# A four-layer FP32 model on one core: VectorE in place of GpSimd makes the low part of each FFN step's product

## The reference

```python
def conv_ffn(h, w_in, conv_w, conv_b, w_out):
    z = causal_dwconv(h @ w_in, conv_w, conv_b)
    u, g = jnp.split(z, 2, axis=-1)
    return (jax.nn.gelu(g) * u) @ w_out
```

```python
    h = rms_norm_2(x, g_ffn)
    a = depthwise_conv(h @ w_ffn_gate, conv_w, conv_b)
    x = x + (jax.nn.gelu(a) * (h @ w_ffn_up)) @ w_ffn_down
```

## Time and profile before

| what | value |
|---|---|
| median of 3 runs | 1607.45 us (1607.23 to 1610.52) |
| the profiled execution, its own time | 1609.04 us |
| its span, first to last instruction | 1607.2 us |
| TensorE matmuls, busy | 1558.6 us, 97% |
| VectorE, busy | 1139.6 us, 71% |
| ScalarE, busy | 908.7 us, 57% |
| GpSimd, busy | 163.4 us, 10%, of which y_lo<-qk 112.5 us in 53 instructions (44 of them in the FFNs) |
| granted clock of TensorE, mean | 0.990 |

### The profile page before, as it was taken

How to read it: one execution, slowest core, us unless ns; L and a number is a source line. 1 busy time by engine, 2 the same in 40 slices (tenths; PEclk the granted TensorE clock), 3 DMA queues, 4 the chain that set the end, 5 groups by cost and what they waited for, 6 DMA issues and landing times.

```text
span 1607.2 us, 30225 instructions
## 1 busy us (share of the span) xinstructions
PE 1558.6 (97%) x12828; PEld 1507.2 (94%) x12828; DVE 1139.6 (71%) x1366; ACT 908.7 (57%) x1207; POOL 163.4 (10%) x94
## 2 busy tenths in 40 slices
PE   7889999998899999999999999998999999999998
PEld 7879999998899999899899999998989989999998
DVE  6638876877888777768647876668677647777566
ACT  6436645677757656646554744456645645645444
POOL 0130112101012110000012010010000012010010
PEclk9989999999999999999999999999999999999999
DMA  9325555444455545432335455544533234565552
GB/s 319 114 83 186 197 188 176 165 142 141 146 183 185 205 164 187 155 131 103 111 124 182 147 205 183 195 172 153 188 133 106 106 106 141 181 210 183 183 186 76
DMA packets 38268, 258.73 MB, mean 161 GB/s; under 512 B 4752, under 2 KB 5392, under 8 KB 7568
## 3 DMA queue, kind: packets, MB, share of 16 engines
q1 hardware_dynamic: 37728, 255.33, 45.8%
q10 hardware_dynamic: 432, 1.84, 0.3%
HBM read 256.10 MB, written 1.05 MB: 160 GB/s over the span
## 4 chain that ended last, share of the span: by engine, by line
PE 77%; issue 10%; DVE 6%; ACT 5%; POOL 1%; DMA 1%; SPq 0%; POOLq 0%; ACTq 0%; DVEq 0%
PE bank L1610 23%; PE bank L1612 22%; PE bank L1611 22%; PE bank L1887 3%; PE bank L1846 3%; DVE w_lo L948 2%; ACT w_hi L474 2%; PE bank L1865 2%; PE bank L1792 1%; DVE qk L1339 1%; PE bank L1819 1%; PE bank L1989 1%; DMA raw<-W 1%; POOL y_lo L1534 1%; DVE h_lo L963 1%
## 5 line engine op out<-in xcount | busy, mean ns | idle before, releaser
L1610 PE MATMUL bank<-h_hi,w_hi 128*128 128x256 f32 x2640 | 751.8, 285 | 19.2 <-DVE h_lo L963 14.7
L1612 PE MATMUL bank<-h_hi,w_lo 128*128 128x256 f32 x2640 | 741.9, 281 | 0.0
L1611 PE MATMUL bank<-h_lo,w_hi 128*128 128x256 f32 x2640 | 741.9, 281 | 0.0
L948 DVE TENSOR_TENSOR w_lo<-raw,w_hi 128x2048 fp32r<-128x2048 f32 x238 | 553.9, 2329 | 199.2 <-ACT w_hi L474 198.3
L474 ACT ACTIVATE w_hi<-raw 128x2048 fp32r<-128x2048 f32 x238 | 455.0, 1912 | 251.8 <-PE bank L1612 250.1
L1610 PEld LDWEIGHTS bank<-h_hi,w_hi 128*128 128x128 f32 x2640 | 498.2, 189 | 32.1 <-issue 12.1
L1612 PEld LDWEIGHTS bank<-h_hi,w_lo 128*128 128x128 f32 x2640 | 501.1, 190 | 0.0
L1611 PEld LDWEIGHTS bank<-h_lo,w_hi 128*128 128x128 f32 x2640 | 498.0, 189 | 0.3
L1610 PE MATMUL bank<-y_hi,w_hi 128*128 128x256 f32 x1040 | 295.6, 284 | 2.7 <-POOL y_lo L1534 2.6
L1612 PE MATMUL bank<-y_hi,w_lo 128*128 128x256 f32 x1040 | 292.2, 281 | 0.0
L1611 PE MATMUL bank<-y_lo,w_hi 128*128 128x256 f32 x1040 | 292.1, 281 | 0.0
(11 more groups left out here) (219 smaller groups left out, 1350.2 us busy)
## 6 DMA issues: line engine op xcount, KB each, us to landing
raw<-W SPq DMA_DIRECT2D x238, 1024.0 KB, 4.9
wide<-RW ACTq DMA_DIRECT2D x1, 1280.0 KB, 10.0
raw<-W SPq DMA_DIRECT2D x2, 512.0 KB, 5.3
x<-XT SPq DMA_DIRECT2D x4, 256.0 KB, 6.5
OUT<-x SPq DMA_DIRECT2D x4, 256.0 KB, 2.0
wide<-CON SPq DMA_DIRECT2D x1, 768.0 KB, 9.9
val<-PE_T ACTq DMA_DIRECT2D x2, 256.0 KB, 3.1
vec<-VEC SPq DMA_DIRECT2D x1, 390.0 KB, 5.0
```

Source lines behind the costliest of these rows:

```text
L948: V.tensor_tensor(w_lo[:, n0 % NW], raw[:, n0 % NRAW], w_hi[:, n0 % NW].bitcast(F32), ALU.subtract)\
L1610: T.matmul(out, w[0], a[0], start=start, stop=False, **kw)
L1611: T.matmul(out, w[0], a[1], start=False, stop=False, **kw)
L1612: return T.matmul(out, w[1], a[0], start=False, stop=stop, **kw)
```

## The change

```diff
--- before.py
+++ after.py
@@ -1095,6 +1095,10 @@
                         after(u + 1, i)
                     if s0 and s0 != FF_STEPS - 2:
                         after(u + 2, i)
+                    dve.wait_ge(sems["yhi"], done(1))
+                    a = y_slot(s0)
+                    V.tensor_tensor(pair(y_lo[:, a], 0), pair(qk, 3), pair(y_hi[:, a], 0).bitcast(F32), ALU.subtract)\
+                        .then_inc(sems["ffy"], 1)
 
                 for s0 in range(3):
                     step(s0)
@@ -1533,16 +1537,6 @@
 
                 return G.tensor_tensor(dst, src, hi.bitcast(F32), ALU.subtract)
 
-            def ffn(s):
-                f = ffs.index(s)
-                with pool.Fori(0, FF_STEPS - 2) as i:
-                    pool.wait_ge(sems["yhi"], i + (FF_STEPS * f + 1))
-                    low(pair(y_lo[:, 0], 0), pair(qk, 3), pair(y_hi[:, 0], 0)).then_inc(sems["ffy"], 1)
-                for s0 in (FF_STEPS - 2, FF_STEPS - 1):
-                    a = y_slot(s0)
-                    pool.wait_ge(sems["yhi"], FF_STEPS * f + s0 + 1)
-                    low(pair(y_lo[:, a], 0), pair(qk, 3), pair(y_hi[:, a], 0)).then_inc(sems["ffy"], 1)
-
             def to_h(s, src):
                 a = atts.index(s)
                 for j in range(4):
@@ -1580,8 +1574,6 @@
                 if k == "pa":
                     pooling(s)
                     to_h(s, hf)
-                elif k in ("ffn", "hf"):
-                    ffn(s)
                 elif k == "rg":
                     for q in range(RG_STEPS):
                         pool.wait_ge(sems["ryhi"], q + 1)
```

## The result

| | before | changed |
|---|---|---|
| runs | 20 | 20 |
| median | 1610.81 us | 1620.43 us |
| ratio | | 1.0061 [1.0048, 1.0075] |
| profiled execution (its span) | 1609.04 (1607.2) us | 1616.28 (1614.2) us |
| mean granted clock in it | 0.990 | 0.987 |

The changed kernel is slower by 0.61%, 9.8 us (7.7 to 12.1 by the interval). One of the 20 executions before took 2163.79 us; it isn't in the ratio, and moves the median by 0.1 us.

The account below looks back on a forecast made before the run. Matmuls fill 97% of the span, so other engines matter only where TensorE waits. Heads -1.1, tails +6.4, hf0 and hf1 +0.2, clock +5.2 make +10.7 us on 1607.45: forecast 1618 us, 8-in-10 range 1611.5 to 1621.5.

Parts of the forecast that it names:

- Loops, hf0 and hf1 at nothing: Steps in the loops keep their length; hf0 and hf1 lose 0.1 us each, 0.2 together.
- Heads, -1.1 us: First steps of the causal FFNs: shorter waits for y_lo gain 0.4 us in ffn0 and 0.7 in ffn1.
- Tails, 2 x 3.2 us: Steps 9 and 10 of ffn0 and ffn1: TensorE restarts 3.2 us later in each, 6.4 together.
- both parts: Step 9's y_lo delays step 10's scaling, 1.4 us; step 10's y_lo stands behind two splits; together 3.2 us per tail.
- The idle time in ffn1: At ffn1's tail TensorE would idle from 610.01 to 613.8 us, 3.8 us.
- The clock, 2 x 2.6 us: Behind both causal tails' waits the granted clock falls to half, costing 2.6 us each, 5.2 together.
- Relief: Rival: y_lo is never late and all six waits in the causal FFNs go, 1604.9 us; chance 0.02.
- The clock holds: Rival: no clock fall behind one causal tail or both, 1615.6 or 1613.0 us; chance 0.25.
- The rule of the two engines that hold each other up: VectorE and GpSimd exclude each other over SBUF; by it alone the change gains, as every y_lo wait goes.
- Pace: Rival: faster matmul pace behind ffn0's tail pays off, chance 0.02; likelier ffn1 stays slow, 2.8 us more, in the range only.

Follow-up runs that it names:

- e4: Kernel before, with only the y_lo of steps 9 and 10 of ffn0 and ffn1 moved to VectorE; 1617.20 us, ratio 1.0065 to the kernel before.
- e7: e5 with the y_lo of ffn1's steps 3, 5 and 7 back on GpSimd; 1606.48 us, ratio 0.9994 to the kernel before.
- e8: e5 with one more TensorE wait, for VectorE's scaling, in ffn1's step 4; 1606.32 us, ratio 0.9993 to the kernel before.
- e5: Changed kernel, causal step 9's y_lo behind step 10's first scaling, y_lo between the splits in causal step 10, hf0 and hf1; 1605.99 us, ratio 0.9988.
- e6: Changed kernel, with step 9's y_lo behind step 10's first scaling in ffn0 and ffn1; 1613.86 us, ratio 1.0041 to the kernel before.
- f1: Changed kernel run again, on one chip with f2; 1617.69 us, ratio 1.0060 to the kernel before.
- f2: e2 run again, on one chip with f1; 1614.14 us, ratio 1.0042 to the kernel before.
- e1: Changed kernel, with step 10's y_lo between its two splits in ffn0 and ffn1; 1611.67 us, ratio 1.0024 to the kernel before.
- e3: Changed kernel, with the y_lo of steps 9 and 10 of ffn0 and ffn1 back on GpSimd; 1609.91 us, ratio 1.0015 to the kernel before.
- e2: Changed kernel, with 24 unused matmuls ahead of TensorE's wait at each causal tail; 1616.43 us, ratio 1.0056 to the kernel before.
- f4: e5 run again; 1604.87 us, ratio 0.9983 to the kernel before.
- the filled kernel: Changed kernel with 24 unused matmuls ahead of TensorE's wait at each causal tail, run as e2 and f2; ratios 1.0056 and 1.0042.

## Why the prediction was right, and where it was not

Forecast 1618.0 us, or 10.7 us (0.66%) slower; measured 1620.43, and 9.8 us (0.61%) over the kernel before, whose own median lay 3.4 us above the one shown.

- **Loops, hf0 and hf1 at nothing: right.** e4 has 40 of the moves undone and the same ratio within its interval. From stage end to stage end hf1 takes 192.91 us before and 193.01 after, both at the slow pace: 0.1 us, as taken. At hf0's tail VectorE's y_lo ended at 1083.91 and TensorE's gap was 0.25 us, 0.13 more than one matmul; 0.1 was taken.
- **Heads, -1.1 us: a little large.** The gap of 0.50 us at ffn0's step 0 is gone (0.4, as taken). That of ffn1 went from 1.06 to 0.52 us, a gain of 0.55 and not 0.7; e7 and e8, with the gap back at 1.06 and 1.12, reach step 9's product 0.5 and 0.6 us later than e5. Together 0.9.
- **Tails, 2 x 3.2 us: right, with both parts.** The first is 1.39 us in the profile and 1.4 in e6 (1.4 taken). The path from step 9's product to TensorE's restart grew by 3.15 us in both. To the last update of x, a tail without a fall costs 3.2 to 3.3 us.
- **The idle time in ffn1: 3.8 forecast, 3.21 measured.** The sum 610.01 us, at which TensorE would run dry, was taken from an execution in which ffn1 ran at the faster pace. At the slow pace TensorE arrives later at a y_lo that doesn't depend on it. e4, whose ffn1 ran at the faster pace, has a gap of 4.02 us in ffn1 against 3.50 in ffn0. It costs nothing either way, since VectorE's chain sets the restart.
- **The clock, 2 x 2.6 us: the mechanism was right, the size too large.** This is the term of the sum that was mis-sized. I took 5.2 us, the mean of three falls, behind every wait. Measured for the two tails together: 4.2 us in one execution of the changed kernel (2.7 and 1.5) and 1.5 in another (1.5 and nothing), about 2.9 on average, and 4.1 in e4's; and f1 against f2, over all their executions, 3.0 +- 1.3. The wait of 3.12 us without a fall had told of this: a fall is likely behind such a wait, and not certain.
- **The sum as measured:** -0.9 + 6.5 + 0.3 + 2.9 = 8.8 us, of 9.8 [7.7, 12.1] in the one comparison and 9.7 (0.0060 x 1607.59) [6.8, 12.7] in the other. What is missing, 1 us, can't be told from the spread. So it is partly luck that 10.7 came so near: the clock term was 2.3 us too large, and about 1 us came that no term of the sum holds. The same tally (tails, heads, hf0 and hf1) leaves 3 us in e1 (1.1 of 3.9), in e3 (-0.5 of 2.4) and in e2 (5.9 of 9.0), which share their runs of the kernel before, but 1.0 in f2 (5.8 of 6.8) and -1.3 in f4 (-1.4 of -2.7). What this rest is stays open: the slow pace of ffn1 (below) would be 1.9 us in each of them, and a common error of those shared runs would do as well.
- **Rivals.** Relief was there, in the heads, and in e5 it wins, but only with other places in the queue. "The clock holds" was half right in some executions, and the changed kernel's runs spread from 1609.18 us to 1625.41: the shortest had a mean granted clock of 0.991, the two longest 0.983. In its 20 executions time and half-speed time go together (correlation 0.85), and half-speed time has a standard deviation of 8.3 us, 8.8 in f1, against 5.5 and 4.7 in the filled kernel. That the falls at the tails make this spread is likely, but not shown, as only a profile tells where a fall lay. The rule of the two engines that hold each other up (the Trainium skill, "SBUF — State Buffer", "Who interferes with whom") agrees with the trace, 5.60 us for two splits beside GpSimd and 4.62 without. The time differs from it in sign, because the rule is about durations and the loss about order.
- **Pace.** I put 2.8 us for a slow ffn1 into the range. It happened in the profiled execution: from rg's last update of x to ffn1's step 9 product it is 166.74 us before, and 168.60 and 168.66 in e7 and e8, which have the same gap of 1.1 us and the slow pace, so it costs 1.9 us. The counts of 146 and 150 in 17 us overstate the difference; start to start it is 2.3% and not 2.7%. Whether the slow pace is a result of the change is open: see the last section.

## What to carry to other kernels

When work is moved from a nearly idle engine to a busy one, look for the instruction that will stand ahead of it in the busy one's queue and for the one that will stand behind it, at the ends of loops above all, where the order differs from the middle: here 4 of 44 moves made the loss, as far as the ratios can tell, though the operation itself became more than three times as fast at the median. The same move between two other instructions (behind the scaling, and between the splits) turned a ratio of 1.006 into 0.9988 and 0.9983. And measure such a local cost between two marks of one chain in the same execution, for it repeats there to 0.1 us where clock and pace are the same (22.04 and 22.02 in e3, 25.20, 25.21, 25.18 and 25.17 in the filled kernel), where medians of whole runs are not exact to 2 us.

## What was unexpected of the hardware

**The clock falls behind some waits of one length and not behind others.** Idle times of 3.20 to 3.7 us at the tails were followed by a fall five times of six (6.8, 3.4, 6.8, 3.4, 3.4 us and none), those of 1.82 us once of two, those of 0.9 us and less never. All falls at the tails went when TensorE was kept busy through the wait. A fall cost 1.5 us of its 3.4, and 2.7 of its 6.8. The two of 6.8 us began while TensorE was still idle, 0.8 and 0.9 us before its restart; the four of 3.4 us (one of them e6's) began 0.2 to 1.2 us behind the restart. A long idle time isn't needed everywhere: in e1 the clock fell for 3.4 us from 1189.7, where TensorE had no gap above 0.32 us in the 14 us ahead. And the longest falls lie in none of the changed places, but in pa: 13.7 us before and 23.9 us in the changed kernel's profile, which is why the mean clocks of two executions don't tell the price of the tails.

**Two paces at the full clock.** The same stream of matmuls runs at 115.6 or at 118.3 ns from start to start, 2.3% apart, and the changes that I looked at came behind waits. At the start of hf0 the same gap of 0.45 us was followed by the slow pace before and by the fast one after. In the kernel before the faster one held in ffn1; in the changed one ffn1 was slow, and hf0 was fast. The rows after, and at last one of the kernel before:

```profile
550.00:567.00 17.00, 17.00 (x146) 17.00 (x145) 12.71 (x15) 11.13 (x12) 0.00 (x0) 1.00 0.54 184
930.00:947.00 17.00, 17.00 (x149) 17.00 (x148) 15.21 (x16) 10.61 (x10) 0.00 (x0) 1.00 0.62 211
```

```profile
930.00:947.00 17.00, 17.00 (x146) 17.00 (x145) 11.44 (x11) 7.81 (x7) 1.29 (x1) 1.00 0.54 187
```

f1 and the first profile of the changed kernel are one program: f1 had no such stretch in its FFNs, the other all but the first 22 us of hf0, where it is worth 3.6 us, nearly as much as the effects studied here. What picks the pace I couldn't find; e7 and e8 show that restoring one wait's length doesn't. In hf0 and hf1 it differs between profiles of one program. In ffn1 it may have to do with the change: the faster pace held from about 505 us to the tail in the profiles of the two kernels whose loop in ffn1 has all its y_lo on GpSimd (before and e4), and in none of the 12 others. By this count the slow ffn1, 1.9 us, could belong to the change. Against it, e5's and f4's times show no such cost. With one or two profiles of each program it stays open.
